# A hybrid decoder step on one core: key pages and samples' bias rows in two buffers, the next weights later

## What is computed

```python
def fox_decode_attention(q, k_new, v_new, c_new, k_past, v_past, c_past):
    s_past = (einsum('bqhd,bkhd->bhqk', q, k_past) * FOX_SCALE
              + (cq[..., :, None] - c_past.transpose(0, 2, 1)[..., None, :]))
    s_new = (einsum('bqhd,bkhd->bhqk', q, k_new) * FOX_SCALE + (cq[..., :, None] - cq[..., None, :]))
    p = softmax(concatenate([s_past, where(tri, s_new, -inf)], axis=-1), axis=-1)
    return (einsum('bhqk,bkhd->bqhd', p[..., :P], v_past) + einsum('bhqk,bkhd->bqhd', p[..., P:], v_new))
```

## Time and profile before

| | us |
|---|---|
| median of three runs | 1604.79 |
| runs | 1603.96 to 1607.48 |
| the profiled execution | 1599.27 |
| its span | 1597.3 |
| TensorE busy | 1543.9 (97%) |
| VectorE busy | 956.0 (60%) |
| ScalarE busy | 735.3 (46%) |
| GpSimd busy | 428.5 (27%) |
| moved from and to HBM | 172.6 MB, 108 GB/s over the span |

### The profile page before, as it was taken

How to read it: one execution, slowest core, us unless ns; L and a number is a source line. 1 busy time by engine, 2 the same in 40 slices (tenths; PEclk the granted TensorE clock), 3 DMA queues, 4 the chain that set the end, 5 groups by cost and what they waited for, 6 DMA issues and landing times. The chain is left out here.

```text
span 1597.3 us, 36603 instructions
## 1 busy us (share of the span) xinstructions
PE 1543.9 (97%) x13742; PEld 1464.8 (92%) x13742; DVE 956.0 (60%) x1668; ACT 735.3 (46%) x1251; POOL 428.5 (27%) x483
## 2 busy tenths in 40 slices
PE   7999999979999999999999999988999999999997
PEld 7999999959999999999999999655799999999997
DVE  5767667745777677633354444677557776766221
ACT  6444444423446666522244355655434465655110
POOL 1222222223345555101000100122033456551000
PEclk9999999989999999999999999999999999999999
DMA  5222222212223222322333434598522232223330
GB/s 209 68 90 88 82 82 82 82 57 85 79 80 107 86 98 78 102 75 83 92 118 111 140 95 145 175 336 310 183 84 76 78 113 81 103 71 111 93 108 25
DMA packets 52307, 174.17 MB, mean 109 GB/s; under 512 B 7202, under 2 KB 8754, under 8 KB 52194
## 3 DMA queue, kind: packets, MB, share of 16 engines
q1 hardware_dynamic: 47282, 155.46, 29.8%
q0 software_dynamic: 4912, 17.12, 3.0%
HBM read 159.99 MB, written 12.57 MB: 108 GB/s over the span
## 5 line engine op out<-in xcount | busy, mean ns | idle before, releaser
L513 ACT ACTIVATE w_hi<-w_raw 128x1024 fp32r<-128x1024 f32 (+1 forms) x153 | 158.0, 1033 | 299.2 <-PE acc L1945 266.7
L995 DVE TENSOR_TENSOR w_lo<-w_raw,w_hi 128x1024 fp32r<-128x1024 f32 (+1 forms) x151 | 183.1, 1213 | 155.6 <-ACT w_hi L513 152.7
L1945 PE MATMUL acc<-xl,w_hi 128*128 128x288 f32 x1136 | 255.3, 306 | 16.0 <-DVE w_lo L1179 9.9
L1945 PE MATMUL acc<-xh,w_hi 128*128 128x288 f32 x1136 | 243.6, 296 | 0.0
L1945 PE MATMUL acc<-xh,w_lo 128*128 128x288 f32 x1136 | 243.6, 296 | 0.0
L1945 PEld LDWEIGHTS acc<-xl,w_hi 128*128 128x128 f32 x1136 | 182.9, 190 | 24.8 <-DVE w_lo L1179 9.9
L1945 PEld LDWEIGHTS acc<-xh,w_hi 128*128 128x128 f32 x1136 | 183.4, 189 | 0.0
L1945 PEld LDWEIGHTS acc<-xh,w_lo 128*128 128x128 f32 x1136 | 182.9, 189 | 0.0
L2130 PE MATMUL aux<-ffn_xsh,w_lo 128*128 128x288 f32 x512 | 151.0, 295 | 0.0
L2130 PE MATMUL aux<-ffn_xsh,w_hi 128*128 128x288 f32 x512 | 150.9, 295 | 0.0
L1945 PE MATMUL acc<-fgl_gl,w_hi 128*128 128x288 f32 x704 | 150.8, 295 | 0.0
(11 more groups left out here) (326 smaller groups left out, 3328.9 us busy)
## 6 DMA issues: line engine op xcount, KB each, us to landing
w_raw<-w_fi_in SPq DMA_DIRECT2D x88, 512.0 KB, 3.6
w_raw<-w_fo_in SPq DMA_DIRECT2D x32, 512.0 KB, 3.6
dec_Kd<-cache_k_in SPq DMA_DIRECT2D x32, 512.0 KB, 5.3
att_Vd<-cache_v_in SPq DMA_DIRECT2D x32, 512.0 KB, 5.8
w_raw<-w_mix_in SPq DMA_DIRECT2D x31, 512.0 KB, 3.6
w_raw<-w_o_in SPq DMA_DIRECT2D x16, 512.0 KB, 3.6
w_raw<-w_kv_in SPq DMA_DIRECT2D x16, 512.0 KB, 3.6
w_raw<-w_qg_in SPq DMA_DIRECT2D x16, 512.0 KB, 3.6
```

Source lines behind the costliest of these rows:

```text
L513: nc.scalar.activation(w_hi[:, pos.slot % SPL, 0:width], w_raw[:, pos.slot, 0:width], ACT.Copy)\
L995: nc.vector.tensor_tensor(w_lo[:, pos.slot % SPL, 0:width], w_raw[:, pos.slot, 0:width], w_hi[:, pos.slot % SPL, 0:width].bitcast(F32), AL ...
L1945: mm = nc.tensor.matmul(dst[:, hf, 0:HALF], W[:, sp_, 128 * (j0 + j):128 * (j0 + j) + 128], x[:, HALF * hf:HALF * hf + HALF], start=(first ...
```

## The change

The key pages get a second buffer. It is the raw weight memory `w_raw` itself (four slots of 512 KB, as large as four pages): even samples use `Kd`, odd ones `w_raw`. `B` gets a second buffer too. Each transfer of keys or of `B` then waits for the use two samples back, and for the landing of the one before it. SP's order in a step changes from keys, prompt bias, `B`, values to `B`, prompt bias, keys, values, and keys are those of the next sample. The loop over the steps, before in a hardware loop, is now written out. The keys of sample 1 are loaded before the stage, each page after the weight block in its slot has been split. Of the output weights only block 0 is in a raw slot ahead of the stage; block 1 goes to the memory of `sq` and `ssq` (`wo_raw`), blocks 2 and 3 are loaded after the last sample's scores.

```diff
+        sq_at = (nc.sbuf_base + 31) // 32 * 32
-        Og = t4("Og", [P, P]); B = t4("B", [P, T]); NC0 = t4("NC0", [P, 2, P])
+        Og = t4("Og", [P, P]); B = t4("B", [P, 2, T]); NC0 = t4("NC0", [P, 2, P])
+        wo_raw = Region("wo", sq_at)("raw", [P, 1024])
+        key_buf = [Kd, w_raw]
...
             def key_pages(n):
 
                 at = [page(n, j) for j in range(PAGES)]
-                wait(sp, d_ps, n)
-                for j in range(PAGES):
-                    sp.dma_start(Kd[:, j, :], row_of(d["cache_k"], at[j])).then_inc(kd_in, 16)
+                wait(sp, d_ps, n - 1)
+                wait(sp, kd_in, 64 * n)
+                for j in (1, 2, 3, 0):
+                    if n == 1:
+                        sp.wait_ge(lo_done, B_WO1 + 1 if j == 0 else B_QG + 13 + j)
+                    sp.dma_start(key_buf[n % 2][:, j, :], row_of(d["cache_k"], at[j])).then_inc(kd_in, 16)
...
             def sample_bias(n):
 
-                wait(sp, dmx_ok, n)
-                sp.dma_start(B[:], d["c_samp"][bass.ds(FOX * n, FOX)].unsqueeze(1).to_broadcast([FOX, DSEQ, T])).then_inc(b_in, 16)
+                wait(sp, dmx_ok, n - 1)
+                wait(sp, b_in, 16 * n)
+                sp.dma_start(B[:, n % 2], d["c_samp"][bass.ds(FOX * n, FOX)].unsqueeze(1).to_broadcast([FOX, DSEQ, T])).then_inc(b_in, 16)
...
             key_pages(0)
-            for j in range(4):
-                load(Pos(B_WO1 + j), d["w_o1"][j])
+            load(Pos(B_WO1), d["w_o1"][0])
+            key_pages(1)
...
             value_pages(0)
-
-            def decode_loads(n, k, more):
-                key_pages(n)
-                if more:
-                    key_bias(n + 1, k)
-                sample_bias(n)
-                value_pages(n)
-            with sp.Fori(0, 3) as i:
-                decode_loads(2 * i + 1, 0, True)
-                decode_loads(2 * i + 2, 1, True)
-            decode_loads(7, 0, False)
+            sp.wait_ge(kn_ok, 16)
+            sp.dma_start(wo_raw[:], d["w_o1"][1]).then_inc(w_in[(B_WO1 + 1) % RAW], 16)
+            for n in range(1, NSEQ):
+                sample_bias(n)
+                if n < NSEQ - 1:
+                    key_bias(n + 1, (n + 1) % 2)
+                    key_pages(n + 1)
+                value_pages(n)
+            sp.wait_ge(d_ps, NSEQ)
+            for j in range(2, 4):
+                load(Pos(B_WO1 + j), d["w_o1"][j])
...
                 if i == NSEQ - 1:
-                    hi(Pos(B_WO1 + 1))
+                    hi(Pos(B_WO1 + 1), raw=wo_raw)
...
-                    nc.vector.tensor_tensor_reduce(out=sc, in0=sc, in1=B[:], scale=-1.0, scalar=3.0e38,
+                    nc.vector.tensor_tensor_reduce(out=sc, in0=sc, in1=B[:, n % 2], scale=-1.0, scalar=3.0e38,
...
-                nc.gpsimd.tensor_tensor(B[:, SEQ:T], B[:, SEQ:T], own[:, i], ALU.add).then_inc(b_ok, 1)
+                nc.gpsimd.tensor_tensor(B[:, i % 2, SEQ:T], B[:, i % 2, SEQ:T], own[:, i], ALU.add).then_inc(b_ok, 1)
...
-                            keys = KT[:, p, SEQ:T] if new else Kd[:, :, P * p:P * p + P]
+                            keys = KT[:, p, SEQ:T] if new else key_buf[n % 2][:, :, P * p:P * p + P]
```

More of the change, by code:

```diff
@@ L506, in _, with hi @@
         def _(act):
-            def hi(pos, width=1024, ready=None):
+            def hi(pos, width=1024, ready=None, raw=None):
                 if ready is None:
@@ L512, in hi @@
                 act.wait_ge(w_in[pos.slot], 16 * pos.lap + 16)
-                nc.scalar.activation(w_hi[:, pos.slot % SPL, 0:width], w_raw[:, pos.slot, 0:width], ACT.Copy)\
+                nc.scalar.activation(w_hi[:, pos.slot % SPL, 0:width], w_raw[:, pos.slot, 0:width] if raw is None else raw[:], ACT.Copy)\
                     .then_inc(hi_done, 1)
@@ L992, in _, with lo @@
         def _(dve):
-            def lo(pos, width=1024):
+            def lo(pos, width=1024, raw=None):
                 dve.wait_ge(hi_done, pos.b + 1)
-                nc.vector.tensor_tensor(w_lo[:, pos.slot % SPL, 0:width], w_raw[:, pos.slot, 0:width],
+                nc.vector.tensor_tensor(w_lo[:, pos.slot % SPL, 0:width], w_raw[:, pos.slot, 0:width] if raw is None else raw[:],
                                         w_hi[:, pos.slot % SPL, 0:width].bitcast(F32), ALU.subtract).then_inc(lo_done, 1)
@@ L1666, in att @@
                 if i == NSEQ - 1:
-                    lo(Pos(B_WO1 + 1))
+                    lo(Pos(B_WO1 + 1), raw=wo_raw)
                 if not cur:
```

## The result

| | before | after |
|---|---|---|
| median | 1603.59 (6 runs, 1601.88 to 1607.48) | 1592.24 (6 runs, 1590.89 to 1594.09) |
| profiled execution | 1599.27 | 1593.87 |
| its span | 1597.3 | 1591.9 |
| the seven cycles of its attention stage | 106.6 | 98.4 |

(The median before is now 1603.59 instead of 1604.79 us, since three more runs stand beside the three shown above.) Inside the stage the two traces differ by just the 8.2 us of the forecast, and the two profiled executions as a whole by only 5.4 us. So the question is where the other 3 us of the medians come from.

The account below looks back on a forecast made before the run. Late bias rows `B` in three of seven attention cycles, not TensorE or DMA alone, were taken to bound the stage. Gains of 0 + 8.25 + 0 us gave 1604.8 - 8.2 = 1596.6 us, range 1593.5 to 1600.5.

Parts of the forecast that it names:

- What bounds the stage, and the wait that goes: Attention stage: late bias rows `B` hold up TensorE in three of seven cycles; without that wait a cycle takes 14.05 us.
- The size: Whole kernel: cutting three long cycles (16.90, 16.90, 16.60 us) to 14.05 gains 8.25 us; 1604.8 becomes 1596.6 us.
- Rival E: TensorE's half clock after pauses: the change leaves the pause at 1018 to 1020 us and removes others; no chance given.
- Keys in two buffers: Key loads of the attention stage: 14 us more slack, no time gained by itself, but the queue's order is freed.
- What is late next: DMA queue: values keep 3.5 us of slack, 14.1 us of traffic in 14.05 us cycles at 356 GB/s; no stall.
- SP's own time: SP's loads, issues and new waits in each cycle: under 14.6 us at the very most, cost 0.
- Start and tail: Loading `K(1)` before the stage and output weight blocks 2 and 3 after the last scores: cost 0, tail cover 6 us.
- VectorE beside GpSimd: Masks moved to mid-cycle on GpSimd slow VectorE there by between zero and 0.94 us a cycle; taken as 0.
- A: DMA becomes the bound of the attention cycles, at 15.0 us a cycle costing 2.9 to 6.7 us: 1600.8 us; chance 0.09.
- D: Masks block VectorE for their whole length on the path, 12.5 us against 8.2: slower, 1609.1 us; chance 0.06.
- C: The wait only changes its name: something else is as late as `B`, long cycles stay, 1604.8 us; chance 0.05.
- B: Masks cost VectorE 0.6 us in the middle of each of seven cycles, 4.2 us: 1600.8 us; chance 0.08.

Follow-up runs that it names:

- four traces: The kernel before, unchanged, profiled four times: attention stages of 106.6, 110.3, 112.0 and 116.0 us, against 98.4 us after the change.
- first trace: The original profiled execution of the kernel before, with no edit: 1599.27 us, attention stage 106.6 us.
- second trace: The kernel before, unchanged, traced again: median 1604.33 us against 1601.51 us for the same kernel beside it; attention stage 110.3 us.

## Why the prediction was right and wrong

*What bounds the stage, and the wait that goes.* Right. Seven cycles of 14.04 us where 14.05 were forecast; 98.4 us where 98.35 follow from 7 x 14.05.

*The size.* Wrong, and the term that failed is the 8.25 us of the three long cycles. They were priced from the one execution that had no half-clock stretch behind its waits; over four traces they cost 8.2, 11.9, 13.6 and 17.6 us, and the medians moved by 11.35. The base of the sum hid it. "The median of the runs shown is 5.5 above the profiled execution, and I subtract from it" kept those 5.5 us in the forecast as if they had nothing to do with the change. 1.2 us of them went with the three further runs of before. Of the rest most had to do with it: what the other executions lie above the first trace is half-clock time behind the very waits that the change takes away, and longer such waits, both inside the stage (in the three traces seven to eight tenths of it half clock, by the clocks of the timed runs something over half). Nothing in the range stood for that: its low end allowed for cycles of 13.8 us, and none were so short. Rival E saw the place ("removes others, so I give it no case of its own"), left them without a price, and should have been a case on the low side: with the 3.7 us of the second trace it would have given about 1593, with the mean of the four about 1592.

*Keys in two buffers.* That by themselves they shorten nothing is borne out beside the second bias buffer (1591.48 without them, 1592.24 with them); that they are what allows the new order was wrong. With the bias rows in two buffers the keys can stay in one.

*What is late next.* Right for the changed kernel: no wait for values. Slack or rate was larger than computed, since 356 GB/s was the demand of those 14 us and not a ceiling. The bias rows themselves came later than computed: GpSimd begins their mask 6.4 to 8.4 us into the cycle, where 5 to 6 were forecast, so that their slack was about 4 us and not 6.

*SP's own time.* Right at 0 for the change as it is, because nothing in SP's order waits long any more. The kernels with the bias rows in one buffer show the other side: an early wait in that order costs the keys 5 to 6 us.

*Start and tail.* Right. Between the last sample's scores and the end of the span lie 466.9 us before and 466.8 after, so the later weights cost nothing. (The weights' sum was slightly off: 3.1 MB at 356 GB/s from 1132.5 end at 1141.3, not "before 1141".) The first matmul behind the stage comes at 1138.72 and not at 1135.8, since the stage itself begins 2.9 us later in this execution; the code ahead of it is the same, and its trace has 20.5 us of half clock there against 13.7.

```profile
1138.72 44.70 PE acc L1952 x336
```

*VectorE beside GpSimd.* Right at 0: VectorE is busier by 1.2 us in all seven cycles together, no cycle is longer for it, and the scalings at the cycle's end take 1.01 us again, as in the undisturbed line of the earlier trace rows.

*Rivals.* A to D did not come; E did, as said. A's waits are absent from the changed kernel and appear with 512 KB more a cycle. Its 15.0 us a cycle had no row behind it, and the middle of its 2.9 and 6.7 us is 4.8, not 4.2. C was refuted by the cycles, B and D by their length.

## What to carry to other kernels

A profiled execution is one draw: where the timed runs lie some us above it, find out what they spend there before you subtract a gain from their median, above all if TensorE waits in bursts. And trace it more than once: here the first of four traces was the mildest. A wait of 2.5 to 4 us in front of dense matmuls is priced with the half-clock stretch that may follow it, here 2.6 us on top of 2.7; what the wait sets free in the clock only helps where TensorE itself is what the next step waits for. And in an in-order queue move the waits before the buffers: a second buffer on the small, early transfer (288 KB here) did all of it. The second buffer for the 2 MB gave about half when it stood alone with the new order, and beside the small one nothing that could be measured.

## What the runs showed of the hardware

- The same kernel at the same place with waits of 2.62 and 2.71 us kept the full clock in one execution and ran at 0.50 for 6.8 us in another.
- Half-clock time of 6.8 us cost about 2.6 us in a stage where TensorE is busy 13.4 of 14.0 us. At the stage's head 3.4 us of it cost nothing: 5.60 us from the pause's end to the first sample's scores with it, 5.61 without.
- A pause of TensorE of 2.4 us at the same place was followed by half clock in six of twelve traces.
- DMA engines at a share of 1.00 to 1.03 moved 351 to 384 GB/s over windows of 14 us, by what they carried.
- A matmul of fp32 operands, 128 x 128 on 128 columns, took two passes of 0.125 us.
